# Attention stage of a two-model block: heads taken in pairs, projections spread between them, first weights loaded in four transfers

## What is computed

```python
def attention_mixer(x, w_in, sink, rpb, w_out):
    h = x @ w_in
    qa, ka, va, qb, kb, vb = jnp.split(h, [512, 640, 768, 1280, 1792], axis=-1)
    qa, ka = rope(qa), rope(ka)                     # 8 query heads, 2 key/value heads of 64
    oa = windowed_gqa_sink(qa, ka, va, sink)        # softmax over |q - k| <= 128 and a sink term
    ob = neighborhood_attention(qb, kb, vb, rpb)    # 8 heads of 64, a bias table per head
    return jnp.concatenate([oa, ob], axis=-1) @ w_out
x = layer_norm(DN_ALPHA * x + mix, ln1_g[0], ln1_b[0])
x = layer_norm(DN_ALPHA * x + squared_relu_mlp(x, mlp_w1[0], mlp_w2[0]), ln2_g[0], ln2_b[0])
```

## Time and profile before

| | |
|---|---|
| median of 3 runs | 2504.34 us (2500.47 to 2505.55) |
| the profiled execution | 2502.07 us |
| its span, first to last instruction | 2500.3 us |
| TensorE busy | 2403.3 us (96%) |
| VectorE busy | 878.4 us (35%) |
| ScalarE busy | 428.0 us (17%) |
| DMA, mean over the span | 268 GB/s |

### The profile page before, as it was taken

How to read it: one execution, slowest core, us unless ns; L and a number is a source line. 1 busy time by engine, 2 the same in 40 slices (tenths; PEclk the granted TensorE clock), 3 DMA queues, 4 the chain that set the end, 5 groups by cost and what they waited for, 6 DMA issues and landing times.

```text
span 2500.3 us, 24353 instructions
## 1 busy us (share of the span) xinstructions
PE 2403.3 (96%) x10366; PEld 1486.2 (59%) x10366; DVE 878.4 (35%) x1733; ACT 428.0 (17%) x972; POOL 69.0 (3%) x123
## 2 busy tenths in 40 slices
PE   8999999999999999989799999999989979999997
PEld 5558547885585448677455555545867645555553
DVE  2445425667354333452221122222345321222212
ACT  2310003356100010220211111111022011111111
POOL 2000000010100000000000000000000000000000
PEclk9999999999999999999899999999999989999999
DMA  7157756344487643234799999992323479999995
GB/s 268 68 189 299 269 207 222 136 177 161 184 302 269 269 168 109 77 144 165 295 423 429 428 430 428 429 407 110 131 91 136 171 309 429 429 428 429 429 429 236
DMA packets 52552, 669.37 MB, mean 268 GB/s; under 512 B 6993, under 2 KB 7537, under 8 KB 13009
## 3 DMA queue, kind: packets, MB, share of 16 engines
q1 hardware_dynamic: 46080, 649.74, 64.0%
q0 software_dynamic: 6352, 17.95, 2.3%
HBM read 666.50 MB, written 1.16 MB: 267 GB/s over the span
## 4 chain that ended last, share of the span: by engine, by line
PE 92%; DVE 4%; DMA 2%; ACT 1%; issue 0%; POOL 0%; DVEq 0%; SPq 0%; ACTq 0%; POOLq 0%
PE ps L101 89%; DVE arena L117 1%; PE ps L296 1%; DMA arena<-ssm_rows 1%; DVE arena L114 1%; PE ps L2176 1%; DVE arena L110 1%; DMA arena<-in_mla_kv_g 1%; DVE arena L128 1%; DMA ring<-in_attn_w_in 0%; ACT arena L106 0%; DVE arena L125 0%; DMA arena<-in_router_b 0%; PE ps L2158 0%; DVE XTGB L111 0%
## 5 line engine op out<-in xcount | busy, mean ns | idle before, releaser
L101 PE MATMUL ps<-ring,arena 128*64 128x512 f32 (+1 forms) x2392 | 874.1, 592 | 7.1 <-DVE arena L117 3.2
L101 PE MATMUL ps<-arena 128*128 128x128 f32 (+7 forms) x3088 | 861.0, 438 | 17.7 <-DVE arena L110 7.8
L101 PE MATMUL ps<-XTGB,ring 128*128 128x256 f32 x2752 | 609.4, 380 | 0.0
L101 PEld LDWEIGHTS ps<-XTGB,ring 128*128 128x128 f32 x2752 | 519.3, 190 | 79.1 <-issue 6.8
L101 PEld LDWEIGHTS ps<-ring,arena 128*64 128x64 f32 (+1 forms) x2392 | 333.6, 156 | 385.1 <-issue 376.4
L101 PEld LDWEIGHTS ps<-arena 128*64 128x64 f32 (+2 forms) x3088 | 395.2, 167 | 214.6 <-issue 183.5
L117 DVE TENSOR_TENSOR arena<-arena,ps 128x512 f32<-128x512 f32 x152 | 104.6, 688 | 414.1 <-PE ps L101 414.1
L101 PE MATMUL ps<-ring,XTGB 128*128 128x512 f32 (+4 forms) x608 | 231.4, 541 | 12.0 <-DVE XTGB L111 7.8
L117 DVE TENSOR_TENSOR arena<-ps,arena 128x512 f32<-128x512 f32 (+4 forms) x148 | 87.0, 623 | 346.8 <-PE ps L101 335.0
L101 PEld LDWEIGHTS ps<-ring,XTGB 128*128 128x128 f32 x608 | 112.5, 200 | 125.5 <-issue 113.1
L101 PE MATMUL ps<-XTGB,arena 128*64 128x512 f32 x384 | 169.1, 593 | 1.4 <-ACT arena L121 1.4
(11 more groups left out here) (140 smaller groups left out, 771.0 us busy)
## 6 DMA issues: line engine op xcount, KB each, us to landing
ring<-in_exp_w SPq DMA_DIRECT2D x96, 2048.0 KB, 17.8
arena<-in_exp_w SPq DMA_DIRECT2D x72, 2048.0 KB, 19.1
ring<-in_mlp_w SPq DMA_DIRECT2D x32, 2048.0 KB, 7.8
ring<-in_ada_w SPq DMA_DIRECT2D x24, 2048.0 KB, 8.3
XTGB<-in_exp_w SPq DMA_DIRECT2D x24, 2048.0 KB, 16.4
ring<-in_ssm_w_in SPq DMA_DIRECT2D x12, 2048.0 KB, 7.9
ring<-in_w_in SPq DMA_DIRECT2D x12, 2048.0 KB, 7.8
ring<-in_gate_w SPq DMA_DIRECT2D x12, 2048.0 KB, 7.8
```

The source lines that it names most:

```text
L101: return self.e.matmul(o, lhsT=lhsT, rhs=rhs, start=start, stop=stop, skip_group_check=True)
```

## The change

- `scores(i)` now takes heads 2i and 2i+1 together, in two banks; its four matmuls alternate between partitions 0 to 63 and 64 to 127.
- `apply(i)` likewise takes two heads; its four matmuls alternate between output partitions 0 to 63 and 64 to 127 of one bank.
- Eight rounds take the place of nineteen. The table `BETWEEN` gives for each round which projections or output projections stand ahead of `apply(i - 1)` and which behind it.
- `out_b` splits the last 16 matmuls: three of the first bank run ahead of the last `apply`, three of the second behind it.
- All results of `apply` are copied by ScalarE (`heads_out`); VectorE's two scores of a pair come before its two `normalise`.
- `a_s`, `a_p`, `a_pt`, `a_st` have four buffers each. The bias has a place of its own in `arena` and is no longer in the ring, so every later load moves one slot on.
- `aq` comes in four transfers of 512 KB, each with a semaphore, and TensorE waits for each before its two chunks. The halves of x have a semaphore each.

```diff
-        a_s = [arena.get(512) for _ in range(2)]
+        a_s = [arena.get(512) for _ in range(4)]
         a_p = [arena.get(512) for _ in range(4)]
-        a_pt = [arena.get(512) for _ in range(2)]
-        a_st = [arena.get(16) for _ in range(3)]
-        AH = 16
+        a_pt = [arena.get(512) for _ in range(4)]
+        a_st = [arena.get(16) for _ in range(4)]
+        abias = arena.get(8, 512)
+        AH, AP = 16, 8
+        BETWEEN = [((0,), (4,)), ((1,), (5,)), ((8,), ()), ((9,), ()), ((2,), (6,)), ((3,), (7,)), ((10,), (11,)),
+                   ((12,), (13,))]
...
-            slab(sp, "aq", "attn_w_in", 0, 8, 512)
+            i, _ = ring.take("aq")
+            shape["aq"] = (8, 512)
+            src = d["attn_w_in"][0:P * SLAB].rearrange("(p f) -> p f", p=P)
+            for j in range(4):
+                f = slice(j * 1024, (j + 1) * 1024)
+                sp.landed(sp.e.dma_start(ring.bufs[i][:, f], src[:, f]), f"aq{j}", ("aq w", j))
...
-            load(sp, "abias", d["attn_bias"].rearrange("(p f) -> p f", p=P), 8, 512, hold=True)
+            sp.landed(sp.e.dma_start(abias, d["attn_bias"].rearrange("(p h f) -> p h f", p=P, h=8)), "abias", "abias")
...
-            ring.drop("abias")
...
-            gemm_t(pe, ("aq",), "aq", 512, [at("XT", 0, 0), at("XT", 0, 1)])
+            w = weights("aq")
+            for t in range(2):
+                ps = bank(pe, "aq", t)
+                pe.wait_ge(at("XT", 0, t))
+                for c in range(8):
+                    pe.wait_ge(at("aq w", c // 2))
+                    ins = pe.mm(ps, XT[:, c, t * P:(t + 1) * P], w[:, c, :], c == 0, c == 7)
+                pe.then_inc(ins, ("aq", t), *([("free", "aq")] if t else []))
...
+            def out_b(q, cs):
+                w = weights("ao1")
+                pe.wait_ge(at("w", "ao1"))
+                t, n = q // 2, q % 2
+                for c in cs:
+                    pe.wait_ge(at("aOT", 4 + c))
+                    ins = pe.mm(ps_of("ao", q), OT[:, 4 + c, t * P:(t + 1) * P], w[:, c, n * 512:(n + 1) * 512],
+                                False, c == 3)
+                if cs[-1] == 3 and n == 1:
+                    pe.then_inc(ins, ("ao", t), *([("free", "ao1")] if t else []))
...
+            def scores(i):
...
-                p0 = 64 * (h % 2)
-                ps = bank(pe, "as", h)
+                    qa, ka = qbT[:, i - 4, :], kbT[:, i - 4, :]
+                    pe.wait_ge(at("abT", i - 4), at("abT", i))
+                ps = [bank(pe, "as", 2 * i + j) for j in range(2)]
                 for t in range(2):
-                    ins = pe.mm(ps[:, t * T:(t + 1) * T], qa[p0:p0 + 64, t * P:(t + 1) * P], ka[p0:p0 + 64, :],
-                                True, True)
-                pe.then_inc(ins, ("as", h))
+                    for j in range(2):
+                        p0 = slice(64 * j, 64 * j + 64)
+                        ins = pe.mm(ps[j][:, t * T:(t + 1) * T], qa[p0, t * P:(t + 1) * P], ka[p0, :], True, True)
+                        if t:
+                            pe.then_inc(ins, ("as", 2 * i + j))
...
+            def apply(i):
...
                 for kc in range(2):
-                    ins = pe.mm(ps[p0:p0 + 64, 0:T], va[:, kc, :], a_pt[h % 2][:, kc * T:(kc + 1) * T],
-                                kc == 0, kc == 1)
...
+                        pe.wait_ge(at("apt", h))
+                        ins = pe.mm(ps[64 * j:64 * j + 64, 0:T], va[:, kc, :], a_pt[h % 4][:, kc * T:(kc + 1) * T],
+                                    kc == 0, kc == 1)
+                pe.then_inc(ins, ("av", i))
+
+            def between(what):
+                for j in what:
+                    if j < 10:
+                        proj(j)
+                    else:
+                        out_a(j - 10)
+
+            for i in range(AP):
+                scores(i)
+                between(BETWEEN[i][0])
+                if i:
+                    apply(i - 1)
+                between(BETWEEN[i][1])
+                turn_p(2 * i)
+                turn_p(2 * i + 1)
+            out_b(0, (0, 1, 2))
+            apply(AP - 1)
+            out_b(1, (0, 1, 2))
+            out_b(0, (3,))
+            out_b(1, (3,))
+            for q in (2, 3):
+                out_b(q, (0, 1, 2, 3))
...
+            def heads_out(i):
+                act.wait_ge(at("av", i))
+                act.then_inc(act.cp(OT[:, i, :], ps_of("av", i)[:, 0:T]), ("aOT", i), ("read", "av", i))
...
-                    bias = weights("abias")[:, h - 8, :]
-                    v.wait_ge(at("w", "abias"))
+                    bias = abias[:, h - 8, :]
+                    v.wait_ge(at("abias"))
...
-            for i in range(AH + 3):
-                if i < AH:
-                    scores(i)
-                if 1 <= i <= AH:
-                    normalise(i - 1)
-                h = i - 3
-                if h >= 0 and h % 4 == 3:
-                    v.wait_ge(at("av", h))
-                    v.then_inc(v.cp(OT[:, h // 2, :], ps_of("av", h // 2)[:, 0:T]), *aot(h), ("read", "av", h // 2))
+            for i in range(AP):
+                for h in (2 * i, 2 * i + 1):
+                    scores(h)
+                for h in (2 * i, 2 * i + 1):
+                    normalise(h)
```

More of the change, by code:

```diff
@@ L206, in build @@
         sems = {}
[L207 to L208 removed]
+        for name in ("x0", "x1", "aq0", "aq1", "aq2", "aq3", "ident", "rope", "consts", "c", "pos", "gb", "sink", "ssmp", "late", "ada_b", "cols", "mod", "gate_b",
+                     "fox_fb", "mla_g", "abias", "router_b", "srow", "se0", "se1", "se2", "out"):
             sems[name] = ctx.enter_context(nc.semaphore("s_" + name))
@@ L501, in out_a @@
                 ps = bank(pe, "ao", q, hold=True)
-                pe.wait_ge(at("w", "ao0"), at("aOT", 3))
+                pe.wait_ge(at("w", "ao0"), *[at("aOT", c) for c in range(4)])
                 for c in range(4):
@@ L549, in attn_pe @@
-            for i in range(AH + 3):
-                if i < AH:
-                    scores(i)
-                if 2 * i < 10:
-                    proj(2 * i)
-                if 11 <= i < 15:
-                    out_a(i - 11)
-                if 2 <= i < AH + 2:
-                    turn_p(i - 2)
-                if 2 * i + 1 < 10:
-                    proj(2 * i + 1)
-                if i > 2:
-                    apply(i - 3)
-            w = weights("ao1")
-            pe.wait_ge(at("w", "ao1"), at("aOT", 7))
@@ L564, in attn_pe @@
-            for q in range(4):
-                t, n = q // 2, q % 2
-                for c in range(4):
-                    ins = pe.mm(ps_of("ao", q), OT[:, 4 + c, t * P:(t + 1) * P], w[:, c, n * 512:(n + 1) * 512],
-                                False, c == 3)
-                if n == 1:
-                    pe.then_inc(ins, ("ao", t), *([("free", "ao1")] if t else []))
+            def apply(i):
+                ps = bank(pe, "av", i)
+                pe.wait_ge(at("avA" if i < 4 else "avB"))
+                for kc in range(2):
+                    for j in range(2):
+                        h = 2 * i + j
+                        if i < 4:
+                            va = vA[:, :, 64 * (h // 4):64 * (h // 4) + 64]
+                        else:
+                            va = vB[:, :, 64 * (h - 8):64 * (h - 8) + 64]
+                        pe.wait_ge(at("apt", h))
+                        ins = pe.mm(ps[64 * j:64 * j + 64, 0:T], va[:, kc, :], a_pt[h % 4][:, kc * T:(kc + 1) * T],
+                                    kc == 0, kc == 1)
+                pe.then_inc(ins, ("av", i))
@@ L607, in copy_pt, with between @@
                 act.wait_ge(at("at", h))
-                if h >= 2:
-                    act.wait_ge(at("av", h - 2))
-                act.then_inc(act.cp(a_pt[h % 2], ps_of("at", h)), ("apt", h), ("read", "at", h))
-            for i in range(AH + 3):
-                if i < AH:
-                    exps(i)
-                if 2 * i < 10:
-                    proj(2 * i)
-                if 2 <= i < AH + 2:
-                    copy_pt(i - 2)
-                if 2 * i + 1 < 10:
-                    proj(2 * i + 1)
-                h = i - 3
-                if h >= 0 and h % 4 == 1:
-                    act.wait_ge(at("av", h))
-                    act.then_inc(act.cp(OT[:, h // 2, :], ps_of("av", h // 2)[:, 0:T]), *aot(h), ("read", "av", h // 2))
+                if h >= 4:
+                    act.wait_ge(at("av", h // 2 - 2))
+                act.then_inc(act.cp(a_pt[h % 4], ps_of("at", h)), ("apt", h), ("read", "at", h))
+            def heads_out(i):
+                act.wait_ge(at("av", i))
+                act.then_inc(act.cp(OT[:, i, :], ps_of("av", i)[:, 0:T]), ("aOT", i), ("read", "av", i))
+            def between(what):
+                for j in what:
+                    if j < 10:
+                        proj(j)
+            for i in range(AP):
+                exps(2 * i)
+                exps(2 * i + 1)
+                between(BETWEEN[i][0])
```

(9 more changed lines are left out.)

46 lines of the change are left out of this document (11 added, 35 removed).

## The result

The changed kernel takes 2477.61 us in the median (2476.80 to 2477.91, 4 runs) against 2504.61 us (2500.47 to 2505.55, 4 runs) for the kernel before on the same chip: a ratio of 0.9895, 95% interval 0.9878 to 0.9912. Its profiled execution takes 2476.80 us with a span of 2475.0. The forecast was 2479 in a range of 2474 to 2489, and 2476.9 for a profiled execution.

What follows compares the result with a forecast made beforehand. The stage was taken as bound by TensorE's instruction stream, with small holes in its second half. Gains 4.2 + 8.0 + 8.5 + 4.5 = 25.2 us from 2502.07 give 2476.9 profiled; with 2.3 for the median, 2479 us, range 2474 to 2489.

Steps and rivals of the forecast that it cites:

- start: `aq` in four transfers starts behind x's turn, near 9.25 instead of 13.46 us: 4.2 us gained.
- applies in pairs: Two heads' applies on column halves run side by side at about the price of one: 8.0 us gained.
- scores in pairs: Two heads' scores on row halves overlap fully, 1.06 us a pair: 8.5 us gained, bounds none to 8.5.
- order: Of 5.4 us of holes and form changes between first scores and stage end, 0.9 stay: 4.5 us gained.
- bias out of the ring: `ao0`, `ao1` and the first MLP slabs load earlier, but none is waited for: nothing gained.
- The rival with quarters 3.2 us apart: At the start, `aq`'s quarters land late, 10.5 to 20.1 us: gain 1.1 instead of 4.2, 2482 us; chance 0.06.
- the slow stretch of 5.3 us: At the start, the first 5.3 us of unbroken TensorE work go at the lower pace, 0.86 us between records.
- the forecast's lower bound of 3.1: At the start, each quarter takes 2.7 us, the last lands at 18.1, `aq` ends at 26.8: gain 3.1 us.
- the row halves: In the paired scores, full overlap assumed without a measured row pair, the column pair being the nearest row: 8.5 us.
- the rival's working: Row halves of the scores don't run side by side, 2.12 us a pair: gain 16.7, 2487.6 us; chance 0.16.
- a pair's chain: From scores' end to last `normalise`, 6.5 us, covered by TensorE's 8.0 to 8.1; round 0 has 0.6 margin.
- The rival counted only the first: Holes remain in the rounds, TensorE waiting for the slower head: 4 to 5 us lost, 2483.5 us; chance 0.07.

Runs made afterwards that it cites:

- the second trace of the kernel before: The kernel before run again without an edit: 2505.23 us, ratio 1.0003; its profiled run took 2505.66 us.
- the quarters alone: The kernel before with only `aq` changed to four transfers, each waited for by its two chunks: 2496.87 us, ratio 0.9972.
- the run with both gaps filled: The changed kernel with 8 matmuls of ones ahead of x's first turn and 12 between its two turns, sink load moved ahead: 2478.88 us.
- each head's weighted sum in one piece: The changed kernel with a pair's four apply matmuls reordered, both of the even head, then both of the odd one: 2479.08 us.
- The kernel built to have no row pair: The changed kernel with both heads' scores computed from partitions 0 to 63: 2485.64 us, ratio 0.9927.
- the projections used up: The changed kernel with another `BETWEEN` table, the ten projections in rounds 0 to 2 and none in rounds 3 to 5: 2494.59 us.
- the kernel with both: The changed kernel with x's second half loaded behind two quarters of `aq`, plus 8 matmuls of ones ahead of x's first turn and 6 behind: 2481.31 us.
- the dummies ahead of x's first turn alone: The changed kernel with eight matmuls of a tile of ones into an unused bank before x's first turn: 2477.62 us, ratio 0.9899.

## Why the prediction was right

**The sum.** 25.2 us were forecast for a profiled execution, and 2502.07 - 2476.80 = 25.3 were measured. That they agree to 0.1 us is luck. The traces put 24.55 of it into the stage's end, 0.3 more than forecast ahead of the first scores and 1.0 less inside the stage, and 0.75 fell behind the stage, where nothing was forecast; against the second trace of the kernel before the same difference is 28.9. What held is the mechanism, and each term to within 0.8 us:

| term | forecast | measured |
|---|---|---|
| start | 4.2 (3.1 to 5.2) | 4.5 in this trace (39.21 - 34.67); 3.8 over eight traces |
| applies in pairs | 8.0 | 16 x 1.00 - 8 x 1.01 = 7.9 |
| scores in pairs | 8.5 (0 to 8.5) | 16 x 1.06 - 8 x 1.07 = 8.4 |
| order | 4.5 | 3.7, what is left of 20.0 |
| bias out of the ring | 0 | 0 within 0.5 us of median |

**Start.** `aq` began at 9.39 where 9.25 was forecast, and the sum came out. Two steps under it were off, and that neither showed in this trace is luck. The quarters don't come 1.55 us apart but 2.0. With the quarters alone, where the fast pace comes early, TensorE's weight loads wait for the third and the fourth (timeline of the weight loads):

```profile
12.52 0.19 PEld L101 LDWEIGHTS ps<-ring,XTGB 128*128 128x128 f32 x1 [0.34 <-DMA ring<-in_attn_w_in]
...
14.35 0.51 PEld L101 LDWEIGHTS ps<-ring,XTGB 128*128 128x128 f32 x2 [0.35 <-DMA ring<-in_attn_w_in]
...
16.37 0.30 PEld L101 LDWEIGHTS ps<-ring,XTGB 128*128 128x128 f32 x2 [0.65 <-DMA ring<-in_attn_w_in]
```

They land 16.37 - 14.35 = 2.0 us apart, as in the run with both gaps filled, and cost 0.1 and 0.4 us beyond the usual 0.24 between two loads. At the lower pace TensorE needs 3.4 us for a quarter's work, so the changed kernel's trace never met this. The rival with quarters 3.2 us apart did not come true either. The fit in the Trainium skill that it takes its 2 us from (DMA: Bandwidth & Descriptors, anatomy of one DMA) is for transfers that GpSimd issues, and the quarters are SyncE's. And the slow stretch of 5.3 us from the earlier trace rows isn't a constant: it ends at 13.8 us in the changed kernel, 4.4 us into `aq`, at 12.52, 2.4 us into it, with the quarters alone, and at 16.56, 6.0 us into it, with each head's weighted sum in one piece. Eight traces with quarters have their first scores at 34.35 to 36.58, 35.5 in the mean, against 39.21, 39.33 and 39.37 with one transfer. The quarters gain 3.8 us in the mean and 2.7 to 5.0 in single traces; three of the eight lie below the forecast's lower bound of 3.1. The scatter is the landing of x's second half and the moment at which the pace doubles, and the forecast had counted on neither moving so far.

**The pairs.** The unmeasured term was the row halves, and the forecast took the column pair of the earlier trace rows as its nearest row. That held: 1.07 us, and 1.92 with both heads in the same rows. The kernel built to have no row pair took 2485.6 us where the rival's working gave 2487.6: two heads in the same rows, one behind the other, cost 1.92 and not 2.12, so 0.2 us of a single head's 1.06 go into its start or end beside rows of another form. At the efficiency that the Trainium skill (TensorE: Matmul & The Clock Gate, Part 3) gives for four row groups, 0.77, a pair would by estimate have taken 1.06 / 0.77 = 1.4 us (the prediction's 1.3 is a slip, and its 2 us are 2.6). For two halves the trace has 1.07, an efficiency of 0.99 against the 1.06 of one head alone, and of 0.90 against the 1.92 of two in the same rows.

**Order.** 0.8 us less than forecast. Eight pairs 16.6, projections 28.4 and 13.9, the output projection 27.9 and the turns leave 1.0 of the 95.58 us where 0.9 was allowed. The turns are the mis-sized part: from start to start two heads' take 43.71 - 42.75 = 0.96 us here, 0.96 to 1.02 in the first seven rounds and 0.88 in the last, in all 7.75 instead of the 7.0 that 0.44 for each head of the earlier trace rows gives. No hole is left: TensorE's only wait in the stage is the 0.61 us ahead of the first scores, which the kernel before has too.

The forecast put a pair's chain at 6.5 us against a cover of 8.1. Timeline of round 1, the scores done at 44.78, and VectorE's last `normalise`:

```profile
44.88 0.69 DVE L114 SCALAR_TENSOR_TENSOR arena<-ps,c_maska 128x512 f32<-128x512 f32 x1 [2.63 <-PE ps L101]
...
50.46 0.62 DVE L110 TENSOR_SCALAR arena<-arena 128x256 f32<-128x256 f32 x2
```

It ends at 51.08, 6.3 us behind the scores, and `turn_p` starts at 53.00. In round 0 the chain ended at 42.25 and `turn_p` started at 42.75, so 0.5 us of the forecast 0.6 was left. Part of what is missing is a load that the forecast hadn't looked at, the sink's:

```profile
36.04 0.69 DVE L114 SCALAR_TENSOR_TENSOR arena<-ps,c_maska 128x512 f32<-128x512 f32 x1 [1.52 <-DMA arena<-in_attn_sink]
```

VectorE's first score starts 1.37 us after TensorE's here (36.04 - 34.67) and 1.25 in the run with both gaps filled, where the sink is loaded earlier and TensorE is the releaser; so it cost 0.12 us. Before, VectorE waited there for TensorE. The earlier start has come up to a load that was ahead before, and where it lands late it takes from the margin of round 0: with the bias back in the ring VectorE's first score starts 36.15 - 34.37 = 1.78 us after TensorE's, the chain ends at 42.34 and `turn_p` starts at 42.45, so that 0.1 us of margin is left.

**Holes.** That they would come back with the projections used up was shown: 9.1 us of waiting and 7.7 at the lower clock. The rival counted only the first.

**Not settled.** The timed medians give the quarters 6.8 (undone) and 7.8 us (alone), the traces 3.8 to 4.9 at the stage's end. The rest lies behind the stage. From its end to the end of the span the three traces with one transfer take 2345.5, 2347.6 and 2348.9 us, the eight with quarters 2342.8 to 2345.9, in the mean 2344.7 against 2347.3. With 3.8 us at the start that makes 6.4. Whether the quarters bring this or three traces happened to be slower is open, and so is why the pace at the start doubles after 2.4 us of `aq` in one trace and after 6.0 in another.

## What to carry to other kernels

Where a float32 contraction spans 64 rows, or an output 64 columns, put two of them on the two halves of TensorE back to back: for the scores and applies here, of 256 columns, the second head costs 0.01 us instead of 1.06 or 1.00. Spread the work that doesn't depend on a softmax over the rounds so that each has more of it than the chain is long; 9.1 us of holes cost 16.8 here, since the clock fell behind them. And at a start that waits for weights, cut the first transfer and leave it there: filling the gaps only moves the wait to the next transfer.

## What was not expected

- The order within a group of four matmuls makes no difference: AABB runs as fast as ABAB, for row halves (1.07 us) and column halves (1.02 us), though TensorE's program has both of the first head's ahead of the second's.
- The granted clock's column says 1.00 from the first us on, while the records of `aq` stand 0.86 us apart in the first stretch. A window of the changed kernel there:

```profile
11.00:12.00 1.00, 1.00 (x2) 0.34 (x1) 0.00 (x0) 0.07 (x1) 1.00 (x3) 1.00 1.04 352
```

  The window from 16 to 17 us of the kernel with both, shown above, has the same two records under way at 0.50, and with the dummies ahead of x's first turn alone the column says 0.50 from 8 to 14 us. So a column of 1.00 at a program's start does not tell the pace: read it from the spacing of records.
- Two runs of the same program differ by 3.6 us: behind the same holes at 1200 us and again near 1700 the clock comes back some 3.5 us sooner or later, and near 1840 it falls in one run and not in the other.
- Smaller transfers on SyncE's queue changed who else gets served: GpSimd's queue has 21.6% of the packets' time in the first 24 us of the changed kernel and 21.8% with the quarters alone, against 12.7% and 12.6% in the two traces of the kernel before, and the attention mask lands 7.7 us after its issue instead of 11.7. SyncE's packets there are smaller, 1300 for 6.52 MB instead of 933 for 7.49 MB. That may be why the quarters land 2.0 us apart and not 1.55; no run separates the two queues.
